# A decoder trunk on one Trainium2 core: inputs turned on the host, one load queue in order of use, index columns as three chunks of 368

## The reference

```python
h = rmsnorm(x, norm_g)                      # x: 256 tokens x 2048
proj = h @ w_in                             # 2048 x 18512, cut into 17 column sections
y_a = u * (tril(W_s) v + b)      * silu(a_z)   # 8 groups, chunks of 128 tokens
y_b = b_bg * conv3(b_cg * b_x)   * silu(b_z)   # causal, depthwise
score[t,s] = sum_h iw[t,h] * relu(iq[t,h] . ik[s])      # 16 index heads of 64
y_c = softmax(q.k over the 64 best keys + rel_bias[bucket(t-s)]) v * silu(c_z)
m = sum_i sigmoid(g_i) * (y_i @ P_i)
out = rmsnorm(x + m @ w_o, final_g)
```

## Time and profile before

| | |
|---|---|
| median of three runs | 1056.47 us |
| profiled execution | 1056.67 us, of which span 1054.9 us |
| PE busy | 99% of the span |
| DVE, ACT, POOL busy | 60%, 46%, 17% |
| DMA | 225.21 MB moved, 213 GB/s over the span |

### The profile page before, as it was taken

How to read it: one execution, slowest core, us unless ns; L and a number is a source line. 1 busy time by engine, 2 the same in 40 slices (tenths; PEclk the granted TensorE clock), 3 DMA queues, 4 the chain that set the end, 5 groups by cost and what they waited for, 6 DMA issues and landing times.

```text
span 1054.9 us, 13771 instructions
## 1 busy us (share of the span) xinstructions
PE 1044.3 (99%) x4712; PEld 861.6 (82%) x4712; DVE 630.5 (60%) x783; ACT 486.0 (46%) x561; POOL 181.5 (17%) x271
## 2 busy tenths in 40 slices
PE   9999999999999999999999999999999999999997
PEld 7888888888788888888888888888888888888886
DVE  5644555555576544755666675566666566666455
ACT  7444444444453444444444453343436545544443
POOL 1100121111101400132223231233221001111003
PEclk9999999999999999999999999999999999999999
DMA  9676666666666666677777777788877557778653
GB/s 293 206 212 197 200 200 197 190 192 199 197 181 194 190 193 198 209 227 231 216 216 221 221 210 221 210 234 246 268 216 231 192 196 234 226 262 269 212 193 139
DMA packets 114583, 225.21 MB, mean 213 GB/s; under 512 B 11812, under 2 KB 12368, under 8 KB 114160
## 3 DMA queue, kind: packets, MB, share of 16 engines
q1 hardware_dynamic: 104528, 200.43, 62.5%
q0 software_dynamic: 9840, 23.75, 7.8%
q10 hardware_dynamic: 176, 0.53, 0.1%
HBM read 211.56 MB, written 13.12 MB: 213 GB/s over the span
## 4 chain that ended last, share of the span: by engine, by line
PE 97%; DVE 1%; ACT 1%; DMA 0%; issue 0%; SPq 0%; DVEq 0%; ACTq 0%
PE psum L1143 31%; PE psum L1145 31%; PE psum L1144 31%; PE psum L1152 0%; DMA keep<-x 0%; PE psum L1290 0%; PE psum L1247 0%; DVE wl L754 0%; PE psum L1319 0%; PE psum L1246 0%; PE psum L1181 0%; PE psum L1207 0%; PE psum L1209 0%; PE psum L1208 0%; PE psum L1280 0%
## 5 line engine op out<-in xcount | busy, mean ns | idle before, releaser
L754 DVE TENSOR_TENSOR wl<-raw,wh 128x1024 fp32r<-128x1024 f32 x370 | 455.1, 1231 | 394.3 <-ACT wh L509 393.6
L509 ACT CAST wh<-raw 128x1024 fp32r<-128x1024 f32 x370 | 388.9, 1051 | 535.4 <-PE psum L1145 528.9
L1143 PE MATMUL psum<-wh,hh 128*128 128x512 f32 x1268 | 498.6, 393 | 0.2 <-DVE keep L763 0.2
L1145 PE MATMUL psum<-wh,hl 128*128 128x512 f32 x1268 | 493.8, 389 | 0.0
L1144 PE MATMUL psum<-wl,hh 128*128 128x512 f32 x1268 | 493.6, 389 | 0.0
L1143 PEld LDWEIGHTS psum<-wh,hh 128*128 128x128 f32 x1268 | 238.0, 188 | 53.4 <-issue 2.7
L1145 PEld LDWEIGHTS psum<-wh,hl 128*128 128x128 f32 x1268 | 238.0, 188 | 50.2
L1144 PEld LDWEIGHTS psum<-wl,hh 128*128 128x128 f32 x1268 | 238.1, 188 | 48.9
L1143 PE MATMUL psum<-wh,yh 128*128 128x512 f32 x192 | 74.7, 389 | 0.0
L1144 PE MATMUL psum<-wl,yh 128*128 128x512 f32 x192 | 74.7, 389 | 0.0
L1145 PE MATMUL psum<-wh,yl 128*128 128x512 f32 x192 | 74.7, 389 | 0.0
(11 more groups left out here) (176 smaller groups left out, 470.9 us busy)
## 6 DMA issues: line engine op xcount, KB each, us to landing
raw<-w_in SPq DMA_DIRECT2D x288, 512.0 KB, 3.8
raw<-w_o SPq DMA_DIRECT2D x32, 512.0 KB, 3.9
raw<-p_c SPq DMA_DIRECT2D x16, 512.0 KB, 3.8
raw<-p_a SPq DMA_DIRECT2D x16, 512.0 KB, 4.1
raw<-p_b SPq DMA_DIRECT2D x16, 512.0 KB, 4.5
qk_away<-keep POOLq DMA_DIRECT2D x32, 64.0 KB, 3.2
keep<-qk_away POOLq DMA_DIRECT2D x8, 256.0 KB, 3.5
cg_away<-early POOLq DMA_DIRECT2D x32, 64.0 KB, 3.5
```

What stands on the lines that cost most here:

```text
L509: act.copy(wh[:, slot, 0:width], raw[:, slot, 0:width]).then_inc(high_split, 1)
L754: dve.tensor_tensor(wl[:, slot, 0:width], raw[:, slot, 0:width], wh[:, slot, 0:width].bitcast(F32), ALU.subtract).then_inc(low_split, 1)
L1143: pe.matmul(dst[t], h, w_h[:, j], start=start, stop=False)
L1145: mm = pe.matmul(dst[t], l, w_h[:, j], start=False, stop=stop)
```

## The change

- The host also gives x turned (`x_turned`: inputs on partitions, tokens along the row, the turned norm weight in front). `a_ws`, `a_b`, `b_conv` and `norm_g` come turned as well. PE turns nothing of x and of the small tensors any more. x in its first form is still loaded, in eight pieces between the loads of chunk 1, for the sum of squares.
- SP issues x and weights in the order of use; the first two subs' weights come as halves, each with its own semaphore, and PE, ACT and DVE work on them block by block (`early_product`).
- `c_z` leaves PSUM unscaled and is scaled in the Silu. Squares, variance and root move to chunks 1 and 2.
- `i_q`, `i_k` and `i_w` are one stretch of 1104 columns in three chunks of 368 (`width_of`, `queries`). The keys are turned by two small transposes in the first chunk of `SUB2` (`turn_keys`).
- The table of biases is made in the middle of the second chunk of 368. The loop over chunks is written out.

The diff, cut to its core:

```diff
+IQW = 368
+IQ_CHUNKS = 3
+IQ_LAST = 288
-PHASE1 = [(C_Z, 2), (I_Q, 2)]
+PHASE1 = [(C_Z, 2)]
...
+            for g in range(FINE):
+                for k in range(KS):
+                    if KS * g + k < 3:
+                        load_x(KS * g + k)
+                    sp.dma_start(raw[:, g, k * N:(k + 1) * N],
+                                 w_in_v[:, KS * g + k, C_Z:C_Z + N]).then_inc(raw_loaded[g] if k else first_loaded[g], 16)
+            load_x(3)
             load_first(2)
+            load_x(4)
             load_first(3)
-            load_x(3)
-            load_x(4)
+            load_x(5)
+            load_x(6)
             for g in range(RING, SUB):
                 load(g, g % RING, KS * g, w_in_v, C_Z)
-            for n in range(2):
-                sp.wait_ge(low_split, SUB + n - RING + 1)
-                sp.dma_start(raw[:, n, 0:KW * IKW].rearrange("p (k c) -> p k c", k=KW),
-                             w_in_v[:, n * KW:(n + 1) * KW, I_K:I_K + IKW]).then_inc(raw_loaded[n], 16)
             for g in range(SUB):
-                load(SUB1 + SUB + g, (SUB1 + g) % RING, KS * g, w_in_v, C_Z + N)
+                load(SUB + g, g % RING, KS * g, w_in_v, C_Z + N)
+                load_rows(g)
+            for c in range(IQ_CHUNKS):
+                for g in range(SUB):
+                    load(SUB * (2 + c) + g, g % RING, KS * g, w_in_v, I_Q + IQW * c, IQW)
...
-            pool.wait_ge(x_loaded[2], 16)
+            for i in range(2 * T):
+                pool.wait_ge(xn_loaded[i], 32)
             pool.dma_start(rel, rel_bias).then_inc(small_loaded, 16)
...
+            for k in range(FINE * KS):
+                g, i = k // KS, k % KS
+                half = slice(i * N, (i + 1) * N)
+                act.wait_ge(raw_loaded[g] if i else first_loaded[g], 16)
+                act.copy(wh[:, g, half], raw[:, g, half]).then_inc(high_split if i else first_high, 1)
+                if k + 1 < FINE * KS:
+                    high_x(k + 1)
...
+            def early_product(k0, count, slot, wait):
+                w_h, w_l = (w[:, slot].rearrange("p (k c) -> p k c", k=KS)[:, k0 % KS:k0 % KS + count] for w in (wh, wl))
+                high, low = wait
+                tok = [slice(t * P, (t + 1) * P) for t in range(T)]
+                pe.wait_ge(*high)
+                for j in range(count):
+                    pe.wait_ge(*high_of(k0 + j))
                     for t in range(T):
+                        pe.matmul(acc[t], hh[:, k0 + j, tok[t]], w_h[:, j], start=k0 + j == 0, stop=False)
+                pe.wait_ge(*low)
+                ...
+                pe.wait_ge(hl_ready, k0 + count)
+                ...
+            for c in range(1, 5):
+                for g in range(SUB):
+                    product(SUB * c + g, g % RING, g, g == SUB - 1, hh, hl, KS * g, CH1 + c, free=evac,
+                            width=width_of(SUB * c + g))
+                    if c == 3 and g == 2:
+                        pe.wait_ge(small_loaded, 16 * 6)
+                        pe.matmul(bank[3][0:HEADS, 0:SKEW], rel, onehot, start=True, stop=True).then_inc(table_done, 1)
+            def turn_keys():
+                for t in range(T):
+                    pe.wait_ge(evac[t], CH2)
+                for t in range(T):
+                    mm = transpose(bank[4][0:IDX_DIM, t * P:(t + 1) * P], ik_n[:, t])
+                mm.then_inc(ik_done, 1)
+                pe.matmul(bank[5][:, 0:T * IDX_HEADS], flip_s[:], iw_n, start=True, stop=True).then_inc(iwf_done, 1)
...
-                        act.activation(section(keep, CZ), section(keep, CZ), ACT.Silu).then_inc(silu_ready, 1)
+                        for t in range(T):
+                            here = keep[:, t, CZ * N:(CZ + 2) * N]
+                            z = act.activation(here, here, ACT.Silu, scale=inv[:, t:t + 1])
+                        z.then_inc(silu_ready, 1)
```

More of the change, by code:

```diff
@@ L68 @@
 PHASE7 = [(G_B, 2)]
-SUB1 = 2
-SUB2 = SUB1 + 4 * SUB
+SUB1 = 0
+SUB2 = SUB1 + 5 * SUB
 SUB3 = SUB2 + 8 * SUB
@@ L177, in trunk @@
         x_s = section(keep, 4, 4)
-        squared = section(keep, 0, 4)
-        g_s = early[0:KD, 1, N:N + P]
-        g_t = early[:, 1, 2 * N:2 * N + KD]
+        squared = keep[:, 0, 8 * N:16 * N]
+        xg = keep[:, 1, 8 * N:16 * N + KD]
+        g_t = xg[:, 0:KD]
+        x_t = xg[:, KD:].rearrange("p (k t) -> p k t", k=KD)
         one = early[:, 1, 3 * N:3 * N + 1]
         one_root = early[:, 1, 3 * N + 1:3 * N + 2]
[L184 to L193, removed]
         onehot = early[0:BUCKETS, 0, 2560:2560 + SKEW]
@@ new lines, in _, with square @@
+            for j in range(FINE, SUB):
+                for k in range(KS * j, KS * j + KS):
+                    high_x(k)
+                if j >= RING:
+                    act.wait_ge(sub_used, j + 1 - RING)
+                split(j, j % RING, j // RING)
+            def square(i):
+                t, half = i // 2, slice(i % 2 * WIDTH, (i % 2 + 1) * WIDTH)
+                act.wait_ge(xn_loaded[i], 32)
+                act.activation(squared[:, i * WIDTH:(i + 1) * WIDTH], x_s[:, t, half], ACT.Square, scale=D ** -0.5,
+                               accum_out=ssq[:, t, i % 2:i % 2 + 1]).then_inc(sq_done, 1)
@@ L1212, in _ @@
-            mm.then_inc(sub_used, 1)
-            pe.wait_ge(diag_ready, 1 + T)
-            pe.matmul(row_acc, ones, diag, start=True, stop=True).then_inc(row_done, 1)
-            some = KW + TAPS * KW
-            pe.wait_ge(small_loaded, 16 * 6)
-            pe.transpose(bank[1][:, 0:some], small[0:some], ident[0:some, 0:some]).then_inc(small_done, 1)
-            for i in range(2):
-                for j in range(4):
-                    mm = transpose(bank[2 + i][:, j * P:(j + 1) * P], ws_s[:, (4 * i + j) * P:(4 * i + j + 1) * P])
-                mm.then_inc(small_done, 1)
@@ L1223, in _ @@
-            pe.matmul(bank[4][0:HEADS, 0:SKEW], rel, onehot, start=True, stop=True).then_inc(table_done, 1)
-            pe.wait_ge(iws_ready, 1)
-            for t in range(T):
-                mm = pe.transpose(bank[5][:, t * IDX_HEADS:(t + 1) * IDX_HEADS], iw_s[:, t * P:(t + 1) * P],
-                                  ident[IDX_DIM:IKW, IDX_DIM:IKW])
-            mm.then_inc(iwt_done, 1)
-            with pe.Fori(1, 4) as c:
-                for g in range(SUB):
-                    product(SUB1 + SUB * c + g, (SUB1 + g) % RING, g, g == SUB - 1, hh, hl, KS * g, CH1 + c, free=evac)
@@ L1372, in _, with piece_of, width_of @@
                     mm.then_inc(half_done, 1)
+def piece_of(k):
+    return [k < last for first, last in PIECES].index(True)
+def width_of(n):
+    return IQW if 2 * SUB <= n < SUB2 else N
 def paired(n):
```

349 lines of the change are left out of this document (162 added, 187 removed).

## The result

The changed kernel takes 1052.72 us (median; 1051.94 to 1052.97) where the one before takes 1056.47: a ratio of 0.9961 [0.9948, 0.9974]. It is faster by 3.75 us. Forecast were 7.4 us and a range that ends at 1051.4, so the direction was right and half of the gain is missing.

What follows compares the result with a forecast made beforehand. PE, busy 99% of the span, was taken to bound the kernel. Chunk 0 -4.9, index keys -8.4, chunks +4.7, small work +1.2 give -7.4 us: 1049.3 profiled, 1049.1 median, 8-in-10 range 1046.8 to 1051.4.

Steps and rivals of the forecast that it cites:

- Chunk 0: First chunk, the later of two counts: ends at 28.8 us instead of 33.72, 4.9 us gained; bounds 27.7 and 31.
- by supply: Chunk 0 by arriving loads: 4.72 MB through at 15.4 us, sub 4's cast ends at 17.1, chunk ends at 28.3 us.
- by PE alone: Chunk 0 by PE's stream: 4.9 + 96 x 0.2275 + 1.0 to 2.4 for the clock, ending at 27.7 to 29.1 us.
- The early start: Start of chunk 0: products begin at 4.9 us, 3.1 us sooner, right after the warm-up transposes.
- sub 4 lands two us later: Chunk 0's upper bound: late landing of sub 4, or a late clock, makes it end at 31 us.
- At nothing: x by rows: Chunk 1's 256 KB row loads beside each 512 KB sub: 288 GB/s asked, under 351 to 388 seen, no cost.
- slightly worse fit at the chunks' ends: Chunk boundaries, part of the small work added: 1.2 us lost in all, bounds 0.9 and 2.4.
- Clock: First products of chunk 0 run at the 1.2 GHz level until the clock rises: 1.0 to 2.4 us lost.
- Index keys and small work: The stretch from 33.72 to 42.12 us behind chunk 0 goes: 8.4 us gained.
- chunks: One chunk of 512 and three of 368 columns take 70.1 us instead of 65.42: 4.7 us lost.
- rivals 1 and 2: 368-column stage: ring starves (1064 us at 9 us landings), chance 4%; weight loads space matmuls 0.19 us (1055.3), chance 3%.
- rival 3: Start: data or clock come late, chunk 0 ends at 31 to 33 us, total 1051 to 1053; chance 12%.

Runs made afterwards that it cites:

- a0: The changed kernel itself, run and profiled again without any edit: 1052.13 us.
- d1: Changed kernel with ACT and DVE copying chunk 0's accumulators out ahead of the split of sub 10, no load moved: 1050.93 us.
- a1: Changed kernel with the first two subs' weights loaded whole, 512 KB each, instead of in halves: 1051.22 us.
- a3_x_late: Changed kernel with the last piece of turned x (512 KB) issued behind the load of sub 4: 1050.82 us.
- b3_x_half: Changed kernel without loading blocks 8 to 15 of turned x (1 MB); blocks 0 to 7 are used twice: 1050.25 us.
- c4_warm36: Changed kernel with 36 warm-up transposes in place of 15: 1052.28 us.
- b1_three: Changed kernel with first two subs loaded whole, last turned x piece behind sub 4's load, and x rows behind chunk 1's last four subs: 1050.18 us.
- a2: Changed kernel without the loads of x by rows; squares are taken of turned x instead: 1051.28 us.
- b2: Changed kernel with the eight pieces of x by rows issued two behind each of chunk 1's last four subs: 1050.64 us.
- c2: Changed kernel with 8 warm-up transposes in place of 15: 1052.77 us.
- d2: Changed kernel with the edits of b1_three plus chunk 0's accumulators copied out ahead of the split of sub 10: 1050.39 us.
- c3: Changed kernel with the last turned x piece behind sub 4's load and x rows behind chunk 1's last four subs, first subs in halves: 1050.30 us.
- d3: Changed kernel with the edits of c3, turned x laid out contiguously per piece, and chunk 0's accumulators copied ahead of sub 10's split: 1049.83 us.

## Why the prediction was half right

The account of the miss, in the profiled execution: 1.2 us at chunk 0's end, 0.85 at the boundary, 0.6 in the rest; together 2.6.

**Chunk 0: the step that failed.** The forecast took the later of two counts, by supply 28.3 us and by PE alone 27.7 to 29.1, and settled on 28.8. It was 30.04 (29.36 in a0). Both counts were short.

*By supply*, I let 4.72 MB be through at 15.4 us by the windows of before, 0.6 us later with the last engine, and sub 4 be cast from 16.0. It was cast at 17.53 (16.9 to 17.5 in a0 and d1). By the windows of the changed kernel itself the 4.72 MB are through at 16.2, because from 4 to 8 us it moved 240 GB/s and not 351. I had taken 351 from a queue that carried large loads behind each other and POOL's beside it, and used it for one that begins with pieces of 128 to 256 KB at 0.4 to 0.5 us an issue. Whole loads bring 288 to 317 there, the halves 235 to 295; why the rate is low is not shown beyond that. The rest, 0.7 us, is in the 0.6 "with the last engine", for which no row stood: the cast came 1.3 us behind the count of bytes, and just as much in a1 (15.5 and 16.79), where the bytes came as forecast.

*By PE alone*, I left out that PE waits at the first blocks for their splits, and charged only the clock. The time of the 96 matmuls beyond 0.2275 us each, from the starts in the profiles:

| run | first product | 0.43 us apart until | lost ahead of sub 4 | in sub 4 | chunk 0 ends |
|---|---|---|---|---|---|
| changed kernel | 4.91 | – | 2.7 | 0.6 | 30.04 |
| a0_again | 4.88 | – | 2.1 | 0.6 | 29.36 |
| a3_x_late | 4.86 | – | 2.6 | 0 | 29.27 |
| b3_x_half | 4.82 | 7.1 | 2.4 | 0 | 29.06 |
| c4_warm36 | 7.40 | – | 0.5 | 0.5 | 30.28 |
| a1_whole | 5.67 | 9.3 | 1.9 | 0 | 29.41 |
| b1_three | 5.98 | 10.4 | 2.3 | 0 | 30.06 |

So the late sub 4, which the forecast watched, costs 0.5 to 0.6 us, and the waits at the first blocks 2.1 to 2.7. With sub 4 in time the chunk ends at 29.3 (a3) and not at 28.3. The early start was mostly paid back there: 2.5 us later costs 0.2 to 0.9 at the end of the chunk (c4, against the two profiles of the changed kernel). These waits are for ACT's casts and DVE's subtractions, and ACT in turn waited for loads, 1.53 us for the second half sub:

```profile
6.80 0.62 ACT L543 CAST wh<-raw 128x512 fp32r<-128x512 f32 x1 [1.53 <-DMA raw<-w_in]
```

The forecast named "sub 4 lands two us later" as the bound that gives 31, so the size was inside its own bounds, but the range was drawn around the kind case.

**"At nothing: x by rows": the second step that failed.** The sum of rates (288 GB/s asked, 351 to 388 to be had) was right as an average. But ACT's slack at that place is none: sub 10 is cast as soon as it lands, and chunk 0's copy stands behind it. A load of 256 KB ahead in the same queue is 0.7 us (a2). I counted the copies under "slightly worse fit at the chunks' ends" and did not look at which instruction stands ahead of them. Two remedies, later rows or an earlier copy, each close the gap (b2, d1).

**Clock: no effect on the changed kernel that the runs resolve, but one in some of the experiments.** I charged 1.0 to 2.4 us for it, as an addition to PE's own time. In the changed kernel's first profile the clock was at its upper level from 4.91 on (the first two products start 0.33 us apart). In c2 they stood 0.43 apart until 7.5, and chunk 0 ended at 29.41, as in a0: the charge vanished in waits that would have come anyway. The time of c2 isn't told from the changed kernel's, though it is 0.5 us above c4's, with ranges that overlap. Where no waits are left it is not so: in a1, b1 and d2 PE has no pause at all, products stand 0.43 apart until 9.3 to 10.7 us, and the 1.9 to 2.4 us lost are the lower clock and one restart, as large as the charge. They show in b1 and d2, whose `SUB2` starts at 101.35 and 101.36, against 100.79 and 100.08 in c3 and d3; that the medians of b1 and c3 are alike (1050.18 and 1050.30), while b1's profile is its slowest execution, suggests that this differs from one execution to the next.

**Index keys and small work, chunks: right.** 8.4 us went, the stage of 368 columns has 0.1684 us for 0.1677, no wait in it, and its ring held (a median of 3.4 us to landing where 5.8 were allowed); rivals 1 and 2 are out. The Trainium skill's section on the issue gap (TensorE: Matmul & The Clock Gate, Back-to-back issue gap), with 155.8 ns at 368 by its isolated formula, is some 13 ns short of the measured spacing, as the rows had said. Chunks and small work together cost 6.5 us for 5.9: 0.2 by spacing, the rest by restarts (0.31 and 0.28 us for the first matmul of a chunk and behind the table, in place of 0.23 and 0.17) and the turned keys.

The time fell in rival 3, "the early start is not kept", with 1051 to 1053 us and 12%. Its reason, waits of PE for fresh splits and data that come late, is what the runs show; its clock is not, nor its end of chunk 0 at 31 to 33 us. That 1052.7 lies in its range owes 0.85 us to the boundary and 0.6 to the rest, which it did not have. It deserved more: that ACT already waited for a load until 16.66 us stood in the trace of before.

## What to carry to other kernels

An engine that is 99% busy over the whole can still wait for its loads at the start. An earlier first instruction is worth only what the waits behind it leave, so sum those of the first blocks as well as the one load that looks late. Ask of each early load when the last byte ahead of it in its queue lands, and try the sum with the first windows at the lowest rate that similar small loads have shown. A transfer is free only if nothing behind it in the same queue is waited for; look at the one load that follows. Where an engine's in-order program has a copy that frees an accumulator, put it ahead of any instruction that waits for a load.

## What was not expected of the hardware

Narrow matmuls seem to have a floor: with weight loads of 128 columns between them, 80 columns come 0.111 us apart, hardly less than 256 at 0.1197. No run here tells the weight load from another cause. The weight loads last 0.19 us in the trace and overlap, so their duration does not tell the floor. The Trainium skill (TensorE: Matmul & The Clock Gate, LDWEIGHTS) has columns / 1.2 ns for a load, an estimate of 107 ns here, and the spacing at the upper clock agrees with it. And the granted clock fell by half in the middle of that stream and rose only at 115.8 us, 2.7 us after matmuls of 512 columns had come back; 368 columns at 0.168 us held 1.00 for 49.5 us.
